# A fused transformer kernel on one core: output and query weights fetched twice, two queries of tile 0 and two modulation rows moved

## What is computed

```
mod = silu(c) @ w_mod + b_mod                       # six rows of 1024: shift, scale, gate, twice
h  = rms_norm(x) * g * (1 + mod[1]) + mod[0]
... retention (4 heads) and differential attention (4 heads) of h and of the context ...
x  = x + mod[2] * (concat(ret, diff) @ w_out)
h2 = rms_norm(x) * g * (1 + mod[4]) + mod[3]
q  = (h2 @ w_query).reshape(t, 8 heads, 2, 128)
s  = einsum('thpc,hpnc->thpn', q, sub_keys)         # 128 scores in each half
v1, i1 = top_k(s[:, :, 0], 16);  v2, i2 = top_k(s[:, :, 1], 16)
best, pos = top_k(v1[..., :, None] + v2[..., None, :], 16)   # of the 256 pairs
experts = (i1 * 128 + i2)[pos];  gate = softmax(best)
act = gelu(einsum('thkd,td->thk', expert_u[experts], h2))
x  = x + mod[5] * einsum('thk,thkd->td', gate * act, expert_v[experts])
```

## Time and profile before

| | us |
|---|---|
| median of 3 runs | 1975.45 |
| lowest, highest | 1967.47, 1979.41 |
| the profiled execution | 1963.47 |
| its span | 1961.6 |
| PE busy in it | 1651.7 (84%) |
| DVE busy | 748.5 (38%) |
| ACT busy | 464.2 (24%) |
| POOL busy | 295.0 (15%) |
| mean DMA rate | 269 GB/s |

### The profile page before, as it was taken

One profiled execution on the slowest core, in us unless ns is written; L12 is line 12 of the kernel. 1 busy time (PEld: TensorE's weight loads), 2 busy tenths in 40 slices (PEclk: granted clock), 3 DMA queues, 4 the chain that ended last, 5 costly groups with the idle time before them and its releaser, 6 DMA issues.

```text
span 1961.6 us, 16021 instructions
## 1 busy us (share of the span) xinstructions
PE 1651.7 (84%) x5752; PEld 841.4 (43%) x5752; DVE 748.5 (38%) x1829; ACT 464.2 (24%) x1240; POOL 295.0 (15%) x268
## 2 busy tenths in 40 slices
PE   6998876667669986897678887898998969999998
PEld 3444452343334532332223322344444446678853
DVE  3643166535685556566653333121000141200001
ACT  3311143212333223333334331112111021210000
POOL 0000003113433333233332133000000000000000
PEclk9999988789879997998799999899999979999999
DMA  9524317789999999999999999576983303244441
GB/s 356 205 96 172 150 35 311 287 343 349 409 383 395 398 417 411 411 408 411 412 407 378 381 410 405 198 259 201 299 283 138 144 28 129 86 129 154 146 158 57
DMA packets 185055, 527.10 MB, mean 269 GB/s; under 512 B 6880, under 2 KB 74464, under 8 KB 151568
## 3 DMA queue, kind: packets, MB, share of 16 engines
q1 hardware_dynamic: 146672, 251.13, 36.2%
q0 software_dynamic: 37584, 270.75, 34.2%
q10 hardware_dynamic: 720, 4.19, 0.6%
HBM read 525.00 MB, written 1.05 MB: 268 GB/s over the span
## 4 chain that ended last, share of the span: by engine, by line
PE 65%; DMA 19%; DVE 9%; ACT 4%; issue 2%; POOL 1%; SPq 0%; POOLq 0%; DVEq 0%; ACTq 0%
PE bank L1024 13%; PE bank L629 9%; DMA arena<-in_peer_rows,pidx 8%; PE bank L1146 7%; PE bank L741 6%; PE bank L690 4%; PE bank L661 4%; DMA ring<-in_ffn_w_gu 4%; PE bank L1101 3%; PE bank L816 3%; DVE arena L2356 3%; PE bank L672 2%; DMA ring<-in_w_mod 2%; PE bank L988 2%; PE bank L997 2%; DMA ring<-in_peer_w_query 2%
## 5 line engine op out<-in xcount | busy, mean ns | idle before, releaser
L1837 POOL DMA_INDIRECT arena<-in_peer_rows,pidx x256 | 290.2, 1134 | 898.2 <-PE bank L1146 576.8
L1146 PE MATMUL bank<-arena,keep 128*32 128x512 f32 x1024 | 281.0, 706 | 137.8 <-ACT keep L1710 137.5
L2356 DVE SCALAR_TENSOR_TENSOR arena<-arena,ring 128x1024 f32<-128x1024 f32 x256 | 305.0, 1223 | 154.0 <-DMA arena<-in_peer_rows,pidx 153.0
L1024 PE MATMUL bank<-ring,hT_all 128*128 128x512 f32 x608 | 281.5, 621 | 29.2 <-DMA ring<-in_ffn_w_gu 15.5
L1024 PEld LDWEIGHTS bank<-ring,hT_all 128*128 128x128 f32 x608 | 118.6, 199 | 186.2 <-issue 159.6
L1146 PEld LDWEIGHTS bank<-arena,keep 128*32 128x32 f32 x1024 | 53.9, 121 | 320.2 <-ACT keep L1710 191.6
L629 PE MATMUL bank<-hT_all,ring 128*128 128x256 f32 x832 | 182.7, 383 | 1.3 <-ACT hT_all L1351 1.3
L629 PEld LDWEIGHTS bank<-hT_all,ring 128*128 128x128 f32 x832 | 159.7, 192 | 24.1 <-ACT hT_all L1351 1.2
L1697 ACT ACTIVATE pf<-pf 128x2 f32<-128x2 f32 x128 | 25.8, 202 | 376.4 <-DVE arena L2356 376.1
L816 PE MATMUL bank<-hT_all,ring 128*128 128x128 f32 (+1 forms) x384 | 64.9, 332 | 31.8 <-DMA ring<-in_peer_w_query 31.4
L741 PE MATMUL bank<-ring,hT_all 128*128 128x512 f32 x192 | 88.7, 620 | 3.0 <-DVE hT_all L1974 3.0
(11 more groups left out here) (374 smaller groups left out, 1713.2 us busy)
## 6 DMA issues: line engine op xcount, KB each, us to landing
ring<-in_ffn_w_gu SPq DMA_DIRECT2D x66, 1024.0 KB
ring<-in_ffn_w_down SPq DMA_DIRECT2D x13, 2048.0 KB
ring<-in_w_mod SPq DMA_DIRECT2D x12, 2048.0 KB
ring<-in_conv_w_in SPq DMA_DIRECT2D x12, 2048.0 KB
ring<-in_mem_w_kv SPq DMA_DIRECT2D x8, 2048.0 KB
ring<-in_w_in SPq DMA_DIRECT2D x6, 2048.0 KB
ring<-in_mem_w_q SPq DMA_DIRECT2D x6, 2048.0 KB
ring<-in_mem_w_o SPq DMA_DIRECT2D x6, 2048.0 KB
```

Source lines behind the costliest of these rows:

```text
L1024: m = mm(b[:, :], src[:, k], slot8[w][:, k], start=(k == 0), stop=(k == KC - 1))
L1146: m = mm(acc[b][r:r + 32, :], diag[n % 8], vslot[n % SLOTS][:, b * 512:(b + 1) * 512], start=(n % 128 < 4), stop=(n % 128 >= 124))
L1837: nc.gpsimd.indirect_dma_start(out=row_in[n % SLOTS], out_offset=None, in_=a["peer_rows"], in_offset=bass.IndirectOffsetOnAxis(ap=pidx[:, ...
L2356: stt(uslot[n % SLOTS], uslot[n % SLOTS], 1.0, h2g[n % 4], ALU.mult, ALU.mult, accum_out=pact2[:, 16 * (g % 2) + k:16 * (g % 2) + k + 1]). ...
```

## The change

The output weights and the first half of the query weights (heads 0 to 3) are fetched twice: `out` and `wq 0`, `wq 1` for tile 0, `out_again` and `wq_again` for tile 1. So `wq 1` follows when `o0b` is done. The order of the pieces from the 17th on is now `out 1`, `out 0`, `wq 0`, `wq 1`, `out_again 1`, `out_again 0`, `wq_again 0`, `wq_again 1`, `wq 2`, `wq 3`, `mod 10`, `mod 11`. `wq_again 1` may overwrite `out_again 1` as soon as tile 1's output has used its first half (`out_half_used`). Queries q02 and q03 and keys 02 and 03 move from picks 8 to 12 into the first part, among tile 1's attention, on PE, ACT and DVE. The modulation rows 10 and 11 move from picks 20 and 28 to 46 and 48, their broadcasts from 32 and 34 to 50 and 52, and they get buffers of their own; memory squares, mean and g5's move follow by two to four picks.

```diff
@@ -108,10 +108,12 @@
...
         wide(name, a["w_mod" if name == "mod" else "w_in"][0], 512 * c, 512 * (c + 1))
-    tall("out", a["w_out"][0])
-    plan[-2], plan[-1] = plan[-1], plan[-2]
-    for name, c in (("wq", 0), ("wq", 1), ("mod", 10), ("mod", 11), ("wq", 2), ("wq", 3)):
-        wide(name, a["w_mod" if name == "mod" else "peer_w_query"][0], 512 * c, 512 * (c + 1))
+    for name in ("out", "out_again"):
+        tall(name, a["w_out"][0])
+        plan[-2], plan[-1] = plan[-1], plan[-2]
+        wide("wq" if name == "out" else "wq_again", a["peer_w_query"][0], 0, 1024)
+    wide("wq", a["peer_w_query"][0], 1024, 2048)
+    wide("mod", a["w_mod"][0], 512 * 10, 512 * 12)
     for l in range(2):
...
@@ -144,10 +146,11 @@
...
 
-PICK_WORK = {0: ["out 1"], 4: ["out 0"], 8: ["regroup 1", "query q02"], 10: ["keys 02", "query q03"], 12: ["keys 03"], 16: ["h2_turns 1"],
-             18: ["regroup 2", "query q10"], 20: ["keys 10", "query q11", "rows 10"], 22: ["keys 11", "query q12"], 24: ["keys 12", "query q13"],
-             26: ["keys 13", "query q4"], 28: ["keys 04", "keys 14", "rows 11"], 30: ["query q5"], 32: ["keys 05", "keys 15", "row r10"], 34: ["row r11"],
-             36: ["query q6"], 38: ["keys 06", "keys 16"], 42: ["query q7"], 44: ["keys 07", "keys 17"], 56: ["mean nm"]}
+PICK_WORK = {0: ["out 1"], 4: ["out 0"], 8: ["regroup 1"], 16: ["h2_turns 1"],
+             18: ["regroup 2", "query q10"], 20: ["keys 10", "query q11"], 22: ["keys 11", "query q12"], 24: ["keys 12", "query q13"],
+             26: ["keys 13", "query q4"], 28: ["keys 04", "keys 14"], 30: ["query q5"], 32: ["keys 05", "keys 15"],
+             36: ["query q6"], 38: ["keys 06", "keys 16"], 42: ["query q7"], 44: ["keys 07", "keys 17"], 46: ["rows 10"], 48: ["rows 11"],
+             50: ["row r10"], 52: ["row r11"], 58: ["mean nm"]}
 for _c in range(3, 16):
...
@@ -206,7 +209,7 @@
...
-                   ("D", "k00"), ("A", "q01 s13a s13b"), ("D", "g0"), ("A", "e00a e00b e01a e01b"), ("D", "k01"), ("A", "e02a e02b e03a e03b")):
+                   ("D", "k00"), ("A", "q01 s13a s13b"), ("D", "g0"), ("A", "e00a e00b e01a e01b"), ("D", "k01"), ("A", "q02 e02a e02b e03a e03b"), ("D", "k02"), ("A", "q03"), ("D", "k03")):
     UNITS += [(n, _e) for n in _names.split()]
...
@@ -347,7 +350,8 @@
...
         mod_part = {0: 2048, 2: 2560, 1: 3072, 3: 3584}
-        mod_part = {i: s_all[:, mod_part.get(i, 3584):mod_part.get(i, 3584) + 512] for i in range(12)}
+        mod_part = {i: s_all[:, mod_part.get(i, 3584):mod_part.get(i, 3584) + 512] for i in range(10)}
+        mod_part[10], mod_part[11] = mem_all[:, 7424:7936], mem_all[:, 6144:6656]
         tmpA, tmpB = h2_all[:, 0:512], h2_all[:, 512:1024]
...
@@ -493,7 +497,8 @@
...
-                     ("out", 0): "o1b", ("out", 1): "o1b", ("wq", 0): "q11", ("wq", 1): "q13", ("wq", 2): "q5", ("wq", 3): "q7",
+                     ("out", 0): "o0b", ("out", 1): "o0b", ("wq", 0): "q01", ("wq", 1): "q03",
+                     ("out_again", 0): "o1b", ("wq_again", 0): "q11", ("wq_again", 1): "q13", ("wq", 2): "q5", ("wq", 3): "q7",
...
@@ -514,6 +519,8 @@
...
                 eng.wait_ge(turn_ready, turn(f"m{i}") + 1)
+            elif (name, i) == ("out_again", 1):
+                eng.wait_ge(sem("out_half_used"), 1)
             elif (name, i) in last_unit:
...
@@ -789,13 +796,15 @@
...
                     if k % 4 == 0:
-                        w = weights(piece["out", k // 4])
+                        w = weights(piece["out_again" if t else "out", k // 4])
                         turned(turn(("mr" if k == 0 else "md") + str(t)))
...
                             m.then_inc(unit_ready, 1)
+                        elif k == 7 and half and t:
+                            m.then_inc(sem("out_half_used"), 1)
 
...
@@ -805,7 +814,7 @@
...
 
-                w = weights(piece["wq", h // 2])
+                w = weights(piece["wq_again" if name[1] == "1" and len(name) == 3 else "wq", h // 2])
                 b = open_unit(name)
...
@@ -968,14 +977,18 @@
...
             key_scores(0, 1)
+            query("q02", 2, slice(0, P))
             diff_turn(1, 2)
...
             repeat_tokens(0, 3)
+            key_scores(0, 2)
             pe.wait_ge(sem("mix_ret"), 2)
...
             diff_values(1, 2)
+            query("q03", 3, slice(0, P))
             diff_turn(1, 3)
             diff_values(1, 3)
+            key_scores(0, 3)
             pe.wait_ge(sem("mix_diff"), 2)
...
@@ -1576,10 +1589,12 @@
...
             repeat_copy(0, 1)
+            query_copy("q02", ("k00",))
             diff_copy(1, 2)
...
             mix_turn("mr", 1)
+            query_copy("q03", ("k01",))
             diff_copy(1, 3)
...
@@ -1606,12 +1621,12 @@
...
 
-            after = {8: [lambda: h2_square(1), lambda: query_copy("q02", ("k00",))], 10: [lambda: h2_root(1), lambda: query_copy("q03", ("k01",))],
-                     16: [lambda: h2_turn(1)], 18: [lambda: query_copy("q10")], 20: [lambda: query_copy("q11"), lambda: on_mod(10)],
+            after = {8: [lambda: h2_square(1)], 10: [lambda: h2_root(1)],
+                     16: [lambda: h2_turn(1)], 18: [lambda: query_copy("q10")], 20: [lambda: query_copy("q11")],
                      22: [lambda: query_copy("q12", ("k10",))], 24: [lambda: query_copy("q13", ("k11",))],
-                     26: [lambda: query_copy("q4", ("k12",))], 28: [lambda: on_mod(11)], 30: [lambda: query_copy("q5", ("k13",))],
-                     36: [lambda: query_copy("q6", ("k14",))], 42: [lambda: query_copy("q7", ("k15",))],
-                     50: [memory_squares, g5_move], 60: [memory_root]}
+                     26: [lambda: query_copy("q4", ("k12",))], 30: [lambda: query_copy("q5", ("k13",))],
+                     36: [lambda: query_copy("q6", ("k14",))], 42: [lambda: query_copy("q7", ("k15",))], 46: [lambda: on_mod(10)], 48: [lambda: on_mod(11)],
+                     54: [memory_squares, g5_move], 60: [memory_root]}
             for j in range(16):
...
@@ -2340,8 +2355,10 @@
...
             diff_copy(1, 2)
+            key_copy(0, 2)
             mix_turn("mr", 1)
             diff_copy(1, 3)
+            key_copy(0, 3)
             mix_diff(1, 3)
...
@@ -2391,13 +2408,14 @@
...
-                    (0, 2): [lambda: select(1), lambda: h2_mean(1), lambda: key_copy(0, 2), lambda: half_top(2, 0), lambda: half_top(2, 1), lambda: best_pairs(2)],
-                    (0, 3): [lambda: h2_apply(1), lambda: key_copy(0, 3), lambda: pair_rows(2), lambda: spread(2)],
-                    (1, 0): [lambda: h2_turn(1)], (1, 1): [lambda: key_copy(1, 0), lambda: key_copy(1, 1), lambda: on_mod(10)],
-                    (1, 2): [lambda: key_copy(1, 2), lambda: key_copy(1, 3)], (1, 3): [lambda: key_copy(0, 4), lambda: key_copy(1, 4), lambda: on_mod(11)],
-                    (2, 0): [lambda: key_copy(0, 5), lambda: key_copy(1, 5), lambda: late_row(0)],
-                    (2, 1): [lambda: late_row(1), lambda: key_copy(0, 6), lambda: key_copy(1, 6)], (2, 3): [lambda: key_copy(0, 7), lambda: key_copy(1, 7)],
-                    (3, 1): [set_ones], (3, 3): [memory_mean],
+                    (0, 2): [lambda: select(1), lambda: h2_mean(1), lambda: half_top(2, 0), lambda: half_top(2, 1), lambda: best_pairs(2)],
+                    (0, 3): [lambda: h2_apply(1), lambda: pair_rows(2), lambda: spread(2)],
+                    (1, 0): [lambda: h2_turn(1)], (1, 1): [lambda: key_copy(1, 0), lambda: key_copy(1, 1)],
+                    (1, 2): [lambda: key_copy(1, 2), lambda: key_copy(1, 3)], (1, 3): [lambda: key_copy(0, 4), lambda: key_copy(1, 4)],
+                    (2, 0): [lambda: key_copy(0, 5), lambda: key_copy(1, 5)],
+                    (2, 1): [lambda: key_copy(0, 6), lambda: key_copy(1, 6)], (2, 3): [lambda: key_copy(0, 7), lambda: key_copy(1, 7), lambda: on_mod(10)],
+                    (3, 0): [lambda: on_mod(11)],
+                    (3, 1): [lambda: late_row(0), lambda: late_row(1), set_ones], (3, 3): [memory_mean],
...
```

## The result

| | before | after |
|---|---|---|
| median, us (4 runs each) | 1977.43 | 1948.12 |
| lowest, highest | 1967.47, 1979.52 | 1943.58, 1949.65 |
| the profiled execution | 1963.47 | 1947.34 |
| its span | 1961.6 | 1945.5 |

The ratio of after to before is 0.9857, 95% interval 0.9829 to 0.9885: faster by 1.4%, or 29 us. Two later comparisons gave 0.9867 and 0.9888 (26 and 21 us).

The account below looks back on a forecast made before the run. It took the expert stage to be bound by DMA, with 39.3 us of transfers lost. Winning 19.3 us, less 8.2 in the first part, gave 11 us off the 1975.45 median: 1964 us, range 1949 to 1982.

Parts of the forecast that it names:

- What bounds the kernel: Expert stage: bound by DMA except at its beginning; 39.3 us of transfer time lost from 302.5 to 577.5 us.
- The first part: Before the third gather: q02, q03 and their keys added on PE delay it by 8.2 us, bounds 6 and 12.
- The weights: Early pieces go out where DMA is nearly idle and are free; wq_again 0 costs nothing, bounds 0 and 5.1 us.
- Rows 10 and 11: Moved to picks 46 and 48: DVE's wait for row 11 falls from 14.5 us to about 2.
- The sum of the losses: Over 302.5 to 577.5 us: 19.3 of 39.3 us won back, less 8.2 at the start, leaves 11 us.
- 14.4 us at 352.5 to 390: Transfer time lost in that stretch, only partly through q02's wait; 8 us were expected to stay, bounds 0 and 14.4.
- 5.9 us at 465 to 502.5: Transfer time lost where q6 and q7 hold PE 7 us each; 3 us were expected to stay, bounds 0 and 5.9.
- rival B: Expert stage: eight slots stay in flight, DMA is kept full, 20 to 24 us won, about 1953; chance 0.22.
- 10 us in hand at picks 12 to 20: Expert stage, picks 12 to 20: the engines' lead there is only 10 us, an argument against DMA being kept full.
- 41 us that the engines could be ahead by pick 32: Expert stage: shorter DVE waits put engines about 41 us ahead, more than DMA can give, so DMA decides.
- C, the waits move: Groups 2 to 4: PE's diagonal waits grow instead, only the 9.5 us q4 gap is won; 1974 to 1978, chance 0.12.
- D, the bill: Four more pieces, 8.4 MB, cost 20.4 us where transfers are the bound; slower, about 1985, chance 0.08.

Follow-up runs that it names:

- e2: The changed kernel run again with nothing edited; 1951.59 us, ratio to before 0.9867.
- e1: The kernel before run again with nothing edited; 1972.79 us, ratio to before 0.9984.
- e10: The changed kernel run a third time, unedited; 1951.31 us, ratio to before 0.9888.
- e5: The kernel before, with only own buffers for modulation rows 10 and 11 added; 1967.19 us, ratio to before 0.9978.
- e3: The changed kernel with each weight fetched once and q02, q03 back at picks 8 and 10; new order and late rows kept; 1957.38 us, ratio to before 0.9903.
- e8: The changed kernel plus four unread 2 MB pieces behind mod 11, ahead of the memory's own transfer; 1973.87 us, ratio to before 1.0013.
- e11: The changed kernel plus four unread 2 MB pieces, with the memory's own transfer put ahead of them; 1972.76 us, ratio to before 0.9986.
- e6: The changed kernel with rows 10 and 11 back at picks 20 and 28, their pieces ahead of wq 2 and wq 3; 1954.83 us, ratio to before 0.9928.
- e7: The changed kernel with q02, q03 moved to pick 6 and their keys to pick 8; 1950.56 us, ratio to before 0.9891.
- e9: The changed kernel with q02, q03 at pick 6 and their keys at pick 8, run again; 1951.57 us, ratio to before 0.9879.

## Why the prediction came out as it did

**What bounds the kernel: right.** It read 39.3 us of lost transfers in the earlier trace rows, and all of the gain lies in that stretch. The better measure, found only afterwards, is from gather to gather: 35.4 us, of which 3.6 are left.

**The first part: right.** 8.2 us predicted, 8.4 in after, 7.1 in e2, and 8.7 between e1 and e10, the two with the low row from 200 to 290. q02 and q03 took 3.74 us each, and keys 03 went into the wait for `mix_diff` (4.13 before, 3.68 now).

**The weights: right.** The early pieces moved at 144 GB/s where there were 14, and PE waits for none of the query weights. `wq_again 0` went out at 306.03, near the 302 that was expected.

**Rows 10 and 11: right, on the low side.** DVE's wait for row 11 was put at 1 to 3 us; there is none. That wait was worth more than the sum gave it: the buffers alone bring 7 us (e5).

**The sum of the losses: here it failed.** "Of the 14.4 us at 352.5 to 390 ... I leave 8", and "of the 5.9 us at 465 to 502.5 ... 3 stay". Both are 0: 414 and 412 GB/s were measured there. With them at 0 the same sum is 39.3 - 6.6 - 2.4 = 30.3 us won, for 31.0 measured, and less 8.2 it is 22.1, for 22.6 at the 81st gather. That is rival B's number, whose 20 to 24 us were given 0.22; its mechanism, eight slots kept in flight by DVE, no run tests. What was wrong in the path of the two terms is not known equally well.

*The 5.9 us at 465 to 502.5: shown.* I put them down to q6 and q7, which stand in that stretch. e5 leaves both in PE's order and takes away only DVE's wait for row 11, and the rate goes from 347 to 417 GB/s. The loss was the aftermath of a wait that my own chain had at 14.5 us.

*The 14.4 us at 352.5 to 390: in part argued.* I took the work in line (DVE's choice, h2 of tile 1, its turns) for a cause beside the wait for `wq 1`, and set it, with the 10 us in hand at picks 12 to 20, against the 41 us that the engines could be ahead by pick 32. The measured lead at gather 17 is 12.5 us (53.6 us after the third before, 41.1 after), near those 10; yet nothing was lost. What my sum had left out is the backlog. By the windows 17.9 MB were moved from 302.5 to 352.5 in before and 16.7 in after. Both kernels issue 14 gathers in that time (14.8 MB), and beside them after issues three pieces (6.3 MB) and before two (4.2). So some 4.4 MB are outstanding at 352.5 instead of 1.1, about 11 us of transfers instead of 3. In the stretch itself after then moves 15.5 MB and before 9.5: by this estimate 3.3 of the 6.0 MB more are backlog, and 2.1 are the 12 gathers issued in it instead of 10. e10, whose gathers run some 4 us later than after's, issues only 10 there, as before did, and moves 416 GB/s. No run takes the backlog away and leaves the rest, nor the work in line, so the shares stay an estimate; e3, with the wait and two pieces as in before, has the dip (251).

**From the profile to the median: a second, smaller fault.** The spans of the two profiled executions differ by 16.1 us, the last gathers by 22.1, the medians by 21 to 29. The sum of 22 fits the last gathers and the lower end of the medians. The spans are closer since the profile of before had the shortest stretch behind the last gather of all (743.4 us). With the sum right and the median of that day, the forecast would have been 1975.45 - 22 = 1953, in the middle of B, and 5 us above what the first four runs gave; two more sets of runs gave 1951.6 and 1951.3. These two lie inside the stated range, so that the first set fell 1 us below it is scatter; that the gain is 21 to 29 us and not 11 isn't. The prediction also held 1% for about what can be told from no change; the interval of the result reaches 0.3% to either side.

**The rivals.** C, the waits move: PE's wait for diagonals did grow, by 15.8 us, but with the transfers full; it was slack. D, the bill: the price is real (e8, e11: some 20 us for 8.4 MB) and the deciding point was as it said, whether the pieces land inside the stage or before it. Here they land before: 99.2 MB against 98.9. The Trainium skill (DMA: Bandwidth & Descriptors, Issuing engines are not separate DMA queues) states that transfers started by any engine run on the same 16 DMA engines and interleave. The prediction drew from it that more bytes cost time; e8 and e11 agree, where these engines are full, and the change itself shows that bytes moved where they stood at 14 GB/s cost nothing that the distance shows.

**Where the 31 us come from**, by the table's standing time: the buffers 7 (35.4 to 28.0), the order of the pieces with the late rows 9 (to 18.8), the double fetch with the early queries 15 (to 3.6), which costs 8.4 at the start, so 7 net. Approached from the other side, the order with the late rows is 8 (e6). e3, which fetches nothing twice, has three quarters of the net gain: its distance is 17.0 us shorter, of 22.6, and its median 20.4 us below before's, of 26.2. That the double fetch wins anything in the end is shown up to the 81st gather (564.6 in e3; 559.1, 557.2 and 562.1 in the change), and not beyond: the last gathers are at 1199.0 and at 1196.1, 1200.8 and 1197.0, and the intervals of the times overlap (0.9876 to 0.9930 against 0.9836 to 0.9898).

Still open: why an execution has the lower clock from 200 to 290 us or not, what makes the stretches behind the 81st gather vary by 10 us, what share the backlog has in the dip that is gone, and why the first comparison gave 29 us where the later ones gave 26 and 21.

## What to carry to other kernels

Where one resource bounds a stage, choose two events of that resource itself as anchors, and take its bytes, its time and its full rate between them: the time in which it stands is all that can be won, and a wait of another engine is worth only what it takes from it (17 us of PE's wait were 8 here). Don't put a dip down to the work that stands in it; a dip can be the aftermath of an earlier wait, as that at 465 to 502.5 was. And carry the bytes that are outstanding from stretch to stretch, since a backlog of pieces keeps the transfers going while the gathers are late. More bytes are free in a stretch where the transfers are idle and cost their full time in one where they are full, so the same 8.4 MB cost nothing or some 20 us by their place in the queue.

## What the runs showed of the hardware

- Gathers of 8 KB rows with 2 MB pieces among them moved 402 to 407 GB/s over 243 to 269 us at a stretch in the change, e7, e8, e9 and e11, and the rate was about the same with 8 MB more of pieces in it (405 in e8, 403 in e11).
- A 2 MB piece beside gathers takes longer than its bytes: `wq 1` was there 24.2 us after its issue in before and 24.3 in e3, where 2 MB at 412 GB/s are 5.1 us.
- The granted clock from 200 to 290 us is 0.92 to 0.94 in ten profiles and 0.87 to 0.88 in three (before and the change each have both), with 3 to 7 us between them at the third gather; the times of before span 12 to 19 us of 1975.
